# A two-layer hybrid diffusion backbone on one core: waits and orders of the opening and odd stages, and router logits in four column groups with a fold

## The chip, the cores and the metric

The kernel runs on one core of a Trainium2 chip. The metric is the device time of one execution in microseconds (us); lower is better. The core has five engines that run side by side: TensorE (PE in the profile, with its weight loads as PEld), VectorE (DVE), ScalarE (ACT), GpSimd (POOL) and SyncE (SP), which here only issues DMAs. Each engine works through its own instruction stream in order, and streams meet only at semaphores. A wait in a stream therefore also holds back everything behind it in that stream.

## The reference, cut to what matters

```python
for l in range(DEPTH):                                   # DEPTH = 2; 1024 latent and 256 context tokens, D = 1024
    mod = split(s_lat @ ada_w[l] + ada_b[l], 6)          # s_lat = silu(c); the same with s_ctx for the context
    h = modulate(rmsnorm(x, norm_mix_g[l]), mod[0], mod[1])
    if l % 2 == 0:   # even: short gated convolution || bidirectional gated linear attention
        k, v, lr_f, lr_b = split(h @ w_in[:, kv])        # la = log_sigmoid(lr @ decay_up + decay_b) / 16
        ...                                              # b = cumsum of la in chunks of 64; exp(b), exp(-b) scale q, k
    else:            # odd: RG-LRU || spatial gating: mixed = einsum(sg_w, layernorm(gelu(v)))
        ...
    x = x + mod[2] * y
    h = modulate(rmsnorm(x, norm_ffn_g[l]), mod[3], mod[4])
    aff = softmax(h @ w_router)                          # 16 experts; each takes its top-C tokens
    x = x + mod[5] * expert_choice_moe(h, aff, ...)
    ...                                                  # the same for the context in layer 0
return rmsnorm(x_lat, norm_final_g)
```

## The kernel before, in words

The 1280 tokens are ten tiles of 128 (`NT` = 10; eight latent, `TL`, and two of context). All work is one hand-written stream per engine, and the stages follow each other in program order on each of them.

**Opening** (`pe_start` and the start of each engine's block). SP issues fifteen small loads, eight 1 MB pieces of `ada_w` (each 128 rows of 2048) into seven slots, and then four weight units of 512 KB; ACT issues the ten token tiles. PE transposes the small vectors, waits for the silu of the conditioning vectors, and then alternates per tile between eight transposes of a normalised tile (`norm_transposes`, L542) and one `ada` piece (L487). ACT computes squares and roots (`act_square`, L1399, and `act_root`, L819) and copies half of each transposed tile (L853); VectorE takes the reciprocal, scales the tile (`dve_norm`, L906 and L909), and copies the other half (L858). After the tiles, VectorE makes the low halves of four weight units (`dve_weight_low`, L899), copies the modulation sums out of PSUM (`dve_ada_rows`, L919), PE transposes them (`ada_rows`, L496), and VectorE adds the bias and makes the scales (`dve_ada_columns`, L936 and L946). Only then can ACT write the high parts of the modulated features (`act_h_high`, L871) and VectorE their low parts (`dve_h_low`, L882 and L890). PE's `job_pair` (L591 to L593) follows them chunk by chunk: each product is three fp32r matmuls, high by high, low by high and high by low.

**Decays and value tiles of the even layer.** PE makes four decay projections (L630). For each of them VectorE runs `dve_decay_in` (L982, L985), ACT an exp and a log with a table load before each (L975, L976), and VectorE `dve_decay_out` (L993 and a scan, L995 or L997). PE then makes 20 value tiles (`v_tile`, L603 to L605, 24 matmuls each), which alternate between PSUM banks 6 and 7: value tile x waits for the copy of tile x-2, which VectorE makes at L2363. In VectorE's stream all 20 copies stand behind the last `dve_decay_out`.

**Output projection and router** (`pe_wout`, `act_wout`, `dve_wout`, one loop over the tiles in each layer). In step i PE projects tile i (48 matmuls, L783 to L785), transposes the normalised tile i-1 (L542), computes the router logits of tile i-2 (eight fp32 matmuls, L798, with the 128x128 features as the stationary operand and 16 columns of the router moving), and transposes the affinities of tile i-3 (L806). VectorE takes the maximum of the logits (L1272), ACT their exp (L1342). After the last tile VectorE ranks tokens (L1292 to L1297), which gives the experts their tokens. In layer 0 PE also does sixteen late `ada_w` pieces after the loop.

**Odd layer** (`pe_odd`, `act_odd`, `dve_odd`). PE transposes ten tiles, then the four 128x128 spatial weights into PSUM bank 7 (L1949), and then waits for `spatial_weights_copied` before `job_pair`. That copy (L2011) stands in ACT's stream behind all 24 instructions of `act_h_high`. The pair writes PSUM banks 0 to 5; the value tiles, later in the stage, write banks 6 and 7.

## Time and profile before

| what | us |
|---|---|
| median of 3 runs | 2715.66 (2715.24 to 2718.46) |
| profiled execution, its own time | 2716.58 |
| span of the profiled execution | 2714.9 |
| PE busy in the span | 2404.2 |
| DVE busy | 1799.7 |
| ACT busy | 1419.0 |

The page cuts the span into 40 slices and gives for each the busy share of an engine in tenths and the clock that TensorE was granted, also in tenths of full speed. Further views list instructions in order of time, with their duration and the idle time in brackets before them with what ended it; the waits of an engine, summed by what they waited for; and the issues and rates of the DMAs.

### The profile page before, as it was taken

To read this page: it belongs to the slowest core of one execution; us is meant where nothing else is said; L and a number is where in the kernel's file an instruction comes from. 1 tells how busy PE (TensorE), PEld (TensorE's weight loads), DVE (VectorE), ACT (ScalarE), POOL (GpSimd) and SP (SyncE) were. 2 spreads that over 40 slices of the span, in tenths; PEclk is the share of its full clock that TensorE was granted. 3 is DMA by queue.
4 is the path that set the end of the run, shared out by engine and by line. 5 is a ranking of instruction groups with operands and counts; after the bars stand their busy time and mean duration, and the time that the engine had idled before them with its cause. 6 is when DMAs were issued, how large, how long until landed. Compare 5 with 4: busy or idle time off the path is not lost.

```text
span 2714.9 us, 33815 instructions
## 1 busy us (share of the span) xinstructions
PE 2404.2 (89%) x13000; PEld 1835.9 (68%) x13000; DVE 1799.7 (66%) x1986; ACT 1419.0 (52%) x1423; POOL 185.8 (7%) x220
## 2 busy tenths in 40 slices
PE   4799999769958999999999967998792899999994
PEld 3697777658815666666666646777582688888883
DVE  5512121554467788888888755566547799999995
ACT  6400102663415566666666643465441677777774
POOL 0000000000001011110101000000000011111100
PEclk8899999789958999999999977999895899999997
DMA  6014443204374788787778760111333799999995
GB/s 234 24 55 140 151 139 130 117 17 163 140 287 162 297 289 296 288 299 294 286 293 289 281 194 20 36 35 28 133 133 138 281 385 391 389 390 390 389 382 196
DMA packets 186995, 582.35 MB, mean 215 GB/s; under 512 B 13208, under 2 KB 58000, under 8 KB 180496
## 3 DMA queue, kind: packets, MB, share of 16 engines
q1 hardware_dynamic: 171488, 526.43, 51.7%
q0 software_dynamic: 12192, 48.24, 6.5%
q10 hardware_dynamic: 3216, 6.29, 0.6%
q8 instruction: 70, 1.15, 0.2%
q14 instruction: 29, 0.24, 0.0%
HBM read 533.74 MB, written 47.19 MB: 214 GB/s over the span
## 4 chain that ended last, share of the span: by engine, by line
PE 83%; DVE 7%; ACT 4%; DMA 3%; issue 2%; SPq 0%; POOL 0%; POOLq 0%; ACTq 0%; DVEq 0%
PE ps L1503 14%; PE ps L1504 13%; PE ps L1505 13%; PE ps L1516 6%; PE ps L566 5%; PE ps L567 4%; PE ps L568 4%; PE ps L783 2%; PE ps L785 2%; PE ps L784 2%; PE ps L487 1%; PE ps L542 1%; PE ps L798 1%; PE ps L603 1%; PE ps L604 1%
## 5 line engine op out<-in xcount | busy, mean ns | idle before, releaser
L1716 DVE TENSOR_TENSOR R_H_r<-R_M,R_W_r 128x2048 fp32r<-128x2048 f32 x336 | 761.7, 2288 | 145.7 <-ACT R_W_r L1619 145.6
L1619 ACT CAST R_W_r<-R_M 128x2048 fp32r<-128x2048 f32 x336 | 640.2, 1913 | 221.3 <-PE ps L1505 84.3
L1505 PE MATMUL ps<-R_W_r,R_C_r 128*128 128x512 f32 x1536 | 607.2, 395 | 0.0
L1503 PE MATMUL ps<-R_W_r,bc_r 128*128 128x512 f32 x1024 | 413.1, 403 | 13.0 <-DVE R_C_r L1734 9.5
L1504 PE MATMUL ps<-R_H_r,bc_r 128*128 128x512 f32 x1024 | 405.3, 396 | 0.0
L1505 PEld LDWEIGHTS ps<-R_W_r,R_C_r 128*128 128x128 f32 x1536 | 291.0, 189 | 65.1
L566 PE MATMUL ps<-R_H_r,R_W_r 128*128 128x512 f32 (+1 forms) x632 | 234.7, 371 | 16.6 <-DVE R_W_r L899 8.9
L1503 PEld LDWEIGHTS ps<-R_W_r,bc_r 128*128 128x128 f32 x1024 | 194.0, 189 | 70.2 <-issue 16.4
L567 PE MATMUL ps<-R_C_r,R_W_r 128*128 128x512 f32 (+1 forms) x632 | 230.4, 365 | 0.0
L568 PE MATMUL ps<-R_H_r,R_W_r 128*128 128x512 f32 (+1 forms) x632 | 229.7, 363 | 0.0
L1504 PEld LDWEIGHTS ps<-R_H_r,bc_r 128*128 128x128 f32 x1024 | 194.2, 190 | 41.4
L1503 PE MATMUL ps<-R_W_r,R_M_r 128*128 128x512 f32 x512 | 202.3, 395 | 7.0 <-DVE R_C L1806 4.5
L1504 PE MATMUL ps<-R_H_r,R_M_r 128*128 128x512 f32 x512 | 202.0, 395 | 0.0
L899 DVE TENSOR_TENSOR R_W_r<-R_W,R_W_r 128x1024 fp32r<-128x1024 f32 x41 | 49.7, 1223 | 172.9 <-ACT R_W_r L895 172.6
L566 PEld LDWEIGHTS ps<-R_H_r,R_W_r 128*128 128x128 f32 x632 | 120.3, 190 | 57.4 <-issue 30.7
L895 ACT CAST R_W_r<-R_W 128x1024 fp32r<-128x1024 f32 x41 | 42.6, 1047 | 213.7 <-DMA R_W<-in_ev_w_in 199.6
L1516 PE MATMUL ps<-R_M,R_C 128*32 128x512 f32 x1344 | 154.2, 596 | 0.0
L568 PEld LDWEIGHTS ps<-R_H_r,R_W_r 128*128 128x128 f32 x632 | 120.4, 191 | 19.0
L567 PEld LDWEIGHTS ps<-R_C_r,R_W_r 128*128 128x128 f32 x632 | 120.6, 191 | 17.2
L783 PE MATMUL ps<-R_H_r,R_M_r 128*128 128x512 f32 x288 | 115.3, 400 | 15.9 <-DVE R_C_r L1238 15.9
L1503 PEld LDWEIGHTS ps<-R_W_r,R_M_r 128*128 128x128 f32 x512 | 97.8, 191 | 40.5 <-issue 19.8
L1716 DVE TENSOR_TENSOR R_H_r<-R_H,R_W_r 128x2048 fp32r<-128x2048 f32 x48 | 109.8, 2288 | 12.9 <-ACT R_W_r L1619 12.9
(291 smaller groups left out, 3734.1 us busy)
## 6 DMA issues: line engine op xcount, KB each, us to landing
R_M<-in_moe_w_gate SPq DMA_DIRECT2D x114, 1024.0 KB, 8.3
R_M<-in_moe_w_down SPq DMA_DIRECT2D x112, 1024.0 KB, 7.8
R_M<-in_moe_w_up SPq DMA_DIRECT2D x110, 1024.0 KB, 7.5
bc<-in_ada_w SPq DMA_DIRECT2D x24, 1024.0 KB, 4.9
R_H<-in_moe_w_up SPq DMA_DIRECT2D x18, 1024.0 KB, 11.1
R_W<-in_ada_w SPq DMA_DIRECT2D x16, 1024.0 KB, 7.5
R_H<-in_moe_w_down SPq DMA_DIRECT2D x16, 1024.0 KB, 10.2
R_H<-in_moe_w_gate SPq DMA_DIRECT2D x14, 1024.0 KB, 9.6
```

Source lines behind the costliest of these rows:

```text
L566: pe.matmul(o, wh[:, k, :], tokens_of(R_Hr, k, c0, cn), start=(k == 0), stop=False)
L567: pe.matmul(o, wh[:, k, :], tokens_of(R_Cr, k, c0, cn), start=False, stop=False)
L568: ins = pe.matmul(o, wl[:, k, :], tokens_of(R_Hr, k, c0, cn), start=False, stop=(k == KC - 1))
L783: pe.matmul(o, xh, whi_out[:, k, cs], start=(k == 0), stop=False)
L784: pe.matmul(o, xh, wlo_out[:, k, cs], start=False, stop=False)
L785: ins = pe.matmul(o, xl, whi_out[:, k, cs], start=False, stop=(k == KC - 1))
L1503: pe.matmul(o, hi[:, k, :], wh[:, kk, cs], start=(k == 0), stop=False)
L1504: pe.matmul(o, hi[:, k, :], wl[:, kk, cs], start=False, stop=False)
L1505: ins = pe.matmul(o, lo[:, k, 0:P], wh[:, kk, cs], start=False, stop=(k == KC - 1))
L1516: ins = pe.matmul(ps[32 * q:32 * q + C, cbank, :], full[:, 2 * j + kk, P:P + C], w[:, kk, c * BANK:(c + 1) * BANK], start=(j == 0), stop=( ...
L1619: nc.scalar.copy(whi[j], raw[slot + j]).then_inc(unit_high_done, 1)
L1716: nc.vector.tensor_tensor(wlo[j], raw[slot + j], whi[j], ALU.subtract).then_inc(unit_low_done, 1)
```

## The change

Six edits:

- The router's 16 columns per 128 rows are stored 32 apart, with zeros between (a memset on POOL at the start). The features now move (128 columns) and a 128x32 piece of the router is stationary. The eight pieces go to four column groups of TensorE, two to each, and so leave four partial sums of the logits on 128 partitions, transposed. ACT copies them out of PSUM, and one more matmul with `fold` (four 16x16 identities below each other) adds the four parts and turns them back. In the loop this fold is issued one step later, after the first twelve matmuls of the next projection; in the last steps at once.
- In the opening, ACT squares and roots tile 0 before the silu, and the exp and log of the LRU constants move behind the decays; VectorE's use of them moves with them. VectorE builds `fold` in three small adds.
- VectorE copies the modulation sums before the weight units' low halves, and makes two of these (not four) before the modulation columns.
- VectorE's copies of value tiles 0 to 4 are put between the steps of the decays.
- In the odd layer PE waits for the spatial weights' copy only before the first value tile.
- The reads of the logits (L1272, L1342) move to columns 128 to 143 of the same PSUM bank.

```diff
@@ pe_wout
+            def logits_folded(t):
+                pe.wait_ge(logit_parts_copied, r0 + t + 1)
+                pe.matmul(ps[:, 2, P:P + NE], logit_parts[:, :], fold[:, :], start=True, stop=True).then_inc(logits_done, 1)
...
                     for k in range(KC):
+                        if i >= 3 and k == 2:
+                            logits_folded(i - 3)
...
                     for k in range(KC):
-                        ins = pe.matmul(ps[:, 2, 0:NE], hN[l][t % 2][:, k, :], router[:, k * NE:(k + 1) * NE],
-                                        start=(k == 0), stop=(k == KC - 1))
-                    ins.then_inc(logits_done, 1)
+                        q = 32 * (k % 4)
+                        ins = pe.matmul(ps[q:q + 32, 2, 0:P], router3[:, k, :], hN[l][t % 2][:, k, :], start=(k < 4), stop=(k >= 4))
+                    ins.then_inc(logit_parts_done, 1)
+                    if i >= nt - 1:
+                        logits_folded(t)
@@ act_wout, behind act_blocks and ahead of act_square
+                if 2 <= i <= nt + 1:
+                    t = i - 2
+                    act.wait_ge(logit_parts_done, r0 + t + 1)
+                    act.wait_ge(logits_done, r0 + t)
+                    nc.scalar.copy(logit_parts[:, :], ps[:, 2, 0:P]).then_inc(logit_parts_copied, 1)
@@ pe_odd
-            pe.wait_ge(spatial_weights_copied, 1)
...
+                    if b == 0:
+                        pe.wait_ge(spatial_weights_copied, 1)
@@ scalar block
+            act.wait_ge(constants_made, 4)
+            tile_in(act, 0)
+            act_square(act, 0)
+            act_root(act, 0)
             act.wait_ge(vectors_copied, 1)
...
-            act.wait_ge(lru_constants_done, 1)
-            own.do(nc.scalar.activation(lruc[:, 8:16], lruc[:, 8:16], ACT.Exp, scale=-1.0))
-            nc.scalar.activation(lruc[:, 8:16], lruc[:, 8:16], ACT.Ln, bias=1.0).then_inc(lambda_log_done, 1)
@@ vector block
+            dve_ada_rows(dve, 0)
-            for u in range(4):
+            for u in range(2):
                 dve_weight_low(dve, u)
-            dve_ada_rows(dve, 0)
             dve_ada_columns(dve, 0)
```

In the opening, on VectorE, the rows before are these (L858 copies the last tiles, L899 are the four low halves, L919 the copies of the modulation sums, L936 and L946 the columns):

```order
L858 COPY R_C<-ps 128x4x128 [waits normed_transposed] x2
L899 TENSOR_TENSOR R_W_r<-R_W,R_W_r 128x1024 [waits weight_high_done] x4
L919 COPY bc<-ps 2x512 [waits constants_made,ada_unit_used]
L919 COPY bc<-ps 2x512 x3
L936 TENSOR_TENSOR modc<-ps,adab 128x16 [waits ada_rows_transposed]
```

and now, with L872, L913, L933 and L950 in their places:

```order
L872 COPY R_C<-ps 128x4x128 [waits normed_transposed] x2
L933 COPY bc<-ps 2x512 [waits constants_made,ada_unit_used]
L933 COPY bc<-ps 2x512 x3
L913 TENSOR_TENSOR R_W_r<-R_W,R_W_r 128x1024 [waits weight_high_done] x2
L950 TENSOR_TENSOR modc<-ps,adab 128x16 [waits ada_rows_transposed]
```

The copies of the sums moved ahead of the low halves, and two of these moved behind the features' low parts.

In the decays, on VectorE, the rows before from the third `dve_decay_in` on (L993 with the scans L995 and L997 is `dve_decay_out`, L2363 the value tiles' copy):

```order
L982 TENSOR_SCALAR R_M<-ps,vcol 128x1280 [waits job_done]
L985 SCALAR_TENSOR_TENSOR R_W<-R_M 128x1280 [waits job_emptied_by_vector]
L993 SCALAR_TENSOR_TENSOR R_W<-R_M,R_W 128x1280 [waits decay_log_done,constants_made]
L995 SCALAR_TENSOR_TENSOR R_M<-bc,R_W 128x1280 [waits vector_own]
L982 TENSOR_SCALAR R_M<-ps,vcol 128x1280 [waits job_done]
L985 SCALAR_TENSOR_TENSOR R_W<-R_M 128x1280 [waits job_emptied_by_vector]
L993 SCALAR_TENSOR_TENSOR R_W<-R_M,R_W 128x1280 [waits decay_log_done,constants_made]
L997 SCALAR_TENSOR_TENSOR R_M<-bc,R_W 128x1280 [waits vector_own]
L993 SCALAR_TENSOR_TENSOR R_W<-R_M,R_W 128x1280 [waits decay_log_done,constants_made]
L997 SCALAR_TENSOR_TENSOR R_M<-bc,R_W 128x1280 [waits vector_own]
L2363 COPY R_M<-ps 128x256 [waits v_tile_done] x15
```

and now (L996 and L999 are `dve_decay_in`, L1007 and L1009 or L1011 `dve_decay_out`, L1017 the copy), up to the last `dve_decay_out`:

```order
L996 TENSOR_SCALAR R_M<-ps,vcol 128x1280 [waits job_done]
L999 SCALAR_TENSOR_TENSOR R_W<-R_M 128x1280 [waits job_emptied_by_vector]
L1017 COPY R_M<-ps 128x256 [waits v_tile_done]
L1007 SCALAR_TENSOR_TENSOR R_W<-R_M,R_W 128x1280 [waits decay_log_done,constants_made]
L1009 SCALAR_TENSOR_TENSOR R_M<-bc,R_W 128x1280 [waits vector_own]
L1017 COPY R_M<-ps 128x256 [waits v_tile_done]
L996 TENSOR_SCALAR R_M<-ps,vcol 128x1280 [waits job_done]
L999 SCALAR_TENSOR_TENSOR R_W<-R_M 128x1280 [waits job_emptied_by_vector]
L1017 COPY R_M<-ps 128x256 [waits v_tile_done]
L1007 SCALAR_TENSOR_TENSOR R_W<-R_M,R_W 128x1280 [waits decay_log_done,constants_made]
L1011 SCALAR_TENSOR_TENSOR R_M<-bc,R_W 128x1280 [waits vector_own]
L1017 COPY R_M<-ps 128x256 [waits v_tile_done] x2
```

Five copies now stand ahead of the last `dve_decay_out`, and fifteen behind it.

In the odd layer, on PE, before (L1949 transposes the spatial weights, L591 opens the pair):

```order
L1949 MATMUL ps<-ident,R_M 128x128 x3
L591 MATMUL ps<-R_H_r,R_W_r 128x512 [waits job_emptied_by_scalar,job_emptied_by_vector,weight_low_done,spatial_weights_copied,h_low_done,h_written_by_scalar,h_written_by_vector]
L592 MATMUL ps<-R_H_r,R_W_r 128x512
```

and now (L596 opens the pair, L608 the first value tile, 340 rows later):

```order
L1973 MATMUL ps<-ident,R_M 128x128 x3
L596 MATMUL ps<-R_H_r,R_W_r 128x512 [waits job_emptied_by_scalar,job_emptied_by_vector,weight_low_done,h_low_done,h_written_by_scalar,h_written_by_vector]
L597 MATMUL ps<-R_H_r,R_W_r 128x512
...
L608 MATMUL ps<-R_W_r,R_H_r 128x256 [waits weight_low_done,spatial_weights_copied]
```

The wait for the copied spatial weights left the pair and stands on the first value tile.

## Rows read from the trace of the kernel before

**Rows 1.** The page: busy time of PE, and its granted clock in slices.
```profile
PE 2404.2 (89%) x13000; PEld 1835.9 (68%) x13000; DVE 1799.7 (66%) x1986; ACT 1419.0 (52%) x1423; POOL 185.8 (7%) x220
PEclk8899999789958999999999977999895899999997
```

**Rows 2.** Waits of PE, first 190 us: for whom, sum, times, longest.
```profile
PE ps L603 <- DVE R_M L2363: 12.2, 1, 12.2
PE ps L496 <- DVE bc L919: 9.0, 1, 9.0
PE ps L542 <- DVE R_W L909: 8.5, 2, 7.5
```

**Rows 3.** Opening: start, us, engine, line, operation, [idle before]; DMA rate in 1.5 us slices.
```profile
15.62 1.28 ACT L2288 ACT_TABLE_LOAD   x1
19.47 0.29 ACT L819 ACTIVATE st<-st,epsc 128x1 f32<-128x1 f32 x1
20.89 1.94 PE L542 MATMUL ps<-ident,R_W 128*128 128x128 f32 x8 [7.48 <-DVE R_W L909]
38.79 1.04 PE L487 MATMUL ps<-R_M,silc 128*2 128x512 f32 x8
GB/s 0 213 399 261 372 382 398 392 429 399 442 407 412 415 415 421 431 415 418 426 410 426 431 400 309 295 291 290 247 53 0 0 0 0 0 0 0 5 0 0
```

**Rows 4.** Instructions in time, DVE and ACT, modulation rows and columns.
```profile
44.59 4.63 DVE L899 TENSOR_TENSOR R_W_r<-R_W,R_W_r 128x1024 fp32r<-128x1024 f32 x4 [0.87 <-ACT R_W_r L895]
49.14 2.78 DVE L919 COPY bc<-ps 2x512 f32<-2x512 f32 x4
53.13 0.26 DVE L936 TENSOR_TENSOR modc<-ps,adab 128x16 f32<-128x16 f32 x2 [1.21 <-PE ps L496]
```

**Rows 5.** Instructions in time, DVE and PE, decays and value tiles.
```profile
118.63 1.52 DVE L982 TENSOR_SCALAR R_M<-ps,vcol 128x1280 f32<-128x1280 f32 x1
120.19 1.49 DVE L985 SCALAR_TENSOR_TENSOR R_W<-R_M 128x1280 f32<-128x1280 f32 x1
121.60 1.48 DVE L993 SCALAR_TENSOR_TENSOR R_W<-R_M,R_W 128x1280 f32<-128x1280 f32 x1
123.11 2.82 DVE L995 TENSOR_TENSOR_SCAN R_M<-bc,R_W 128x1280 f32<-128x1280 f32 x1
137.78 0.58 PE L603 MATMUL ps<-R_W_r,R_H_r 128*128 128x256 f32 x1 [12.21 <-DVE R_M L2363]
148.68 0.42 DVE L2363 COPY R_M<-ps 128x256 f32<-128x256 f32 x1 [2.46 <-PE ps L605]
```

**Rows 6.** Instructions in time, one step of the router's loop, and an expert stage.
```profile
673.35 1.86 PE L798 MATMUL ps<-router,R_H 128*128 128x16 f32 x16
675.06 0.27 PE L806 MATMUL ps<-ident,sm 128*16 128x128 f32 x1
676.37 0.16 DVE L1272 TENSOR_REDUCE st<-ps 128x1 f32<-128x16 f32 x1
673.55 1.50 ACT L835 ACTIVATE R_H<-ps,modc,scg 128x128 f32<-128x128 f32 x4 [6.57 <-PE ps L542]
877.33 3.64 PE L1516 MATMUL ps<-R_M,R_C 128*32 128x512 f32 x32
880.90 0.51 PE L1503 MATMUL ps<-R_W_r,bc_r 128*128 128x512 f32 x1
878.22 0.13 PEld L1516 LDWEIGHTS ps<-R_M,R_C 128*32 128x32 f32 x4 [0.30 <-issue]
```

**Rows 7.** Instructions in time, PE, behind layer 0's last projection.
```profile
748.77 3.43 PE L798 MATMUL ps<-router,R_H 128*128 128x16 f32 x16
753.15 3.57 PE L798 MATMUL ps<-router,R_H 128*128 128x16 f32 x16 [0.73 <-ACT sm L1342]
```

**Rows 8.** Instructions in time, start of the odd layer's pair: DVE, PE.
```profile
1640.55 0.68 DVE L890 TENSOR_TENSOR R_C_r<-R_C,R_H_r 128x512 fp32r<-128x512 f32 x1
1654.54 0.77 PE L591 MATMUL ps<-R_H_r,R_W_r 128*128 128x512 f32 x1 [15.97 <-DVE R_C_r L890]
```

More of the change, by code:

```diff
@@ L94, in build @@
         st = sb("st", 64)
-        router = sb("router", KC * NE)
+        router = sb("router", KC * 32)
+        router3 = router[:, :].rearrange("p (k e) -> p k e", e=32)
+        fold = sb("fold", NE)
+        logit_parts = sb("logit_parts", P)
         dec = sb("dec", 4 * NCH)
@@ L403, in build @@
         normed_stored = sem("normed_stored")
+        logit_parts_done = sem("logit_parts_done")
+        logit_parts_copied = sem("logit_parts_copied")
         logits_done = sem("logits_done")
@@ L998, in dve_decay_out, with dve_v_copied @@
             ins.then_inc(decays_summed, 1)
+        def dve_v_copied(dve, x):
+            half, t = divmod(x, NT)
+            dve.wait_ge(v_tile_done, x + 1)
+            nc.vector.tensor_copy(vtok[:, t, 256 * half:256 * half + 256], ps[:, 6 + x % 2, 0:256]).then_inc(v_tile_copied, 1)
         def dve_even_job(dve, own, j):
@@ L1271, in dve_wout @@
                     dve.wait_ge(logits_done, r0 + t + 1)
-                    own.do(nc.vector.reduce_max(st[:, b:b + 1], ps[:, 2, 0:NE], AXX))
+                    own.do(nc.vector.reduce_max(st[:, b:b + 1], ps[:, 2, P:P + NE], AXX))
                     nc.vector.tensor_scalar(st[:, b + 1:b + 2], st[:, b:b + 1], -1.0, None, ALU.mult).then_inc(logit_max_done, 1)
@@ L1341, in act_wout @@
                         act.wait_ge(affinities_transposed, r0 + t - 1)
-                    nc.scalar.activation(sm[:, s0:s0 + NE], ps[:, 2, 0:NE], ACT.Exp, bias=st[:, b + 1:b + 2],
+                    nc.scalar.activation(sm[:, s0:s0 + NE], ps[:, 2, P:P + NE], ACT.Exp, bias=st[:, b + 1:b + 2],
                                          accum_out=st[:, b + 2:b + 3]).then_inc(logit_exps_done, 1)
@@ L1392, in sp_wout @@
                 if i == 0:
-                    sp.dma_start(router[:, :].rearrange("p (k e) -> p k e", e=NE),
+                    sp.dma_start(router3[:, :, 0:NE],
                                  I["moe_router"][l].rearrange("(k p) e -> p k e", p=P)).then_inc(lowrank_weights_loaded, 16)
@@ L2176, in _ @@
             pool.wait_ge(constants_made, 1)
+            own.do(pool.memset(router[:, :], 0.0))
             pool.memset(decup[96:128, :], 0.0).then_inc(constants_made, 1)
@@ L2284, in _ @@
                 nc.scalar.activation(s3[:, :, w], vcol[:, VEC[name]:VEC[name] + KC], ACT.Silu).then_inc(cond_silu_done, 1)
[L2286 to L2289 removed]
             for t in range(NT + 1):
[L2291 removed]
+                if 1 <= t < NT:
                     tile_in(act, t)
@@ L2304, in _ @@
                 act_decay(act, own, jobs[j][1])
+            act.wait_ge(lru_constants_done, 1)
+            own.do(nc.scalar.activation(lruc[:, 8:16], lruc[:, 8:16], ACT.Exp, scale=-1.0))
+            nc.scalar.activation(lruc[:, 8:16], lruc[:, 8:16], ACT.Ln, bias=1.0).then_inc(lambda_log_done, 1)
             for u in range(index["cg0"], index["cg0"] + 2):
@@ L2334, in _ @@
             own.do(nc.vector.tensor_scalar(lruc[:, 0:8], lam, -1.0, 0.0, ALU.mult, ALU.max))
-            dve.wait_ge(lambda_log_done, 1)
-            own.do(nc.vector.tensor_tensor(lruc[:, 0:8], lruc[:, 0:8], lruc[:, 8:16], ALU.add))
-            nc.vector.tensor_scalar(lruc[:, 16:24], lruc[:, 0:8], -LRU_C, None, ALU.mult)
-            nc.vector.tensor_scalar(lruc[:, 0:8], lruc[:, 0:8], LRU_C, None, ALU.mult).then_inc(lru_constants_done, 1)
+            dve.wait_ge(constants_made, 1)
+            own.do(nc.vector.tensor_tensor(fold[:, :], ident[:, 0:NE], ident[:, 32:32 + NE], ALU.add))
+            own.do(nc.vector.tensor_tensor(fold[:, :], fold[:, :], ident[:, 64:64 + NE], ALU.add))
+            own.do(nc.vector.tensor_tensor(fold[:, :], fold[:, :], ident[:, 96:96 + NE], ALU.add))
             for t in range(NT + 1):
@@ L2349, in _ @@
             dve_h_low(dve, own, 0)
-            for u in range(4, 7):
+            for u in range(2, 7):
                 dve_weight_low(dve, u)
-            for pd in range(4):
-                dve_decay_in(dve, pd)
-                if pd >= 1:
-                    dve_decay_out(dve, own, pd - 1)
-            dve_decay_out(dve, own, 3)
-            for x in range(2 * NT):
-                half, t = divmod(x, NT)
+            dve_decay_in(dve, 0)
+            dve_decay_in(dve, 1)
+            dve_decay_out(dve, own, 0)
+            dve_decay_in(dve, 2)
+            dve_v_copied(dve, 0)
+            dve_decay_out(dve, own, 1)
+            dve_v_copied(dve, 1)
+            dve_decay_in(dve, 3)
+            dve_v_copied(dve, 2)
+            dve_decay_out(dve, own, 2)
+            dve_v_copied(dve, 3)
+            dve_v_copied(dve, 4)
+            dve_decay_out(dve, own, 3)
+            dve.wait_ge(lambda_log_done, 1)
+            own.do(nc.vector.tensor_tensor(lruc[:, 0:8], lruc[:, 0:8], lruc[:, 8:16], ALU.add))
+            nc.vector.tensor_scalar(lruc[:, 16:24], lruc[:, 0:8], -LRU_C, None, ALU.mult)
+            nc.vector.tensor_scalar(lruc[:, 0:8], lruc[:, 0:8], LRU_C, None, ALU.mult).then_inc(lru_constants_done, 1)
+            for x in range(5, 2 * NT):
                 if x == NT + 5:
@@ L2361, in _ @@
                         dve_weight_low(dve, u)
-                dve.wait_ge(v_tile_done, x + 1)
-                nc.vector.tensor_copy(vtok[:, t, 256 * half:256 * half + 256], ps[:, 6 + x % 2, 0:256]).then_inc(v_tile_copied, 1)
+                dve_v_copied(dve, x)
             for i in range(len(even_late)):
```

2 lines of the change are left out of this document (removed).

## The prediction

> **What bounds the kernel now.** I read the page's engine shares first: PE is busy for 2404.2 of 2714.9 us, the others for at most 1800 [rows 1]. Outside PE's own work there are some 310 us in which it waits, and the slices of its granted clock dip to 0.7 or 0.8 of full speed around the same places. So an edit is worth what it takes from PE's waits, or from PE's work where PE never waits. Then I read the list of PE's waits over the first 190 us: one wait of 12.2 us for the copy of a value tile, one of 9.0 us for the copy of the modulation sums, and 8.5 us for the first normalised tiles [rows 2]. The instructions in order of time give the rest: in the router's loop PE has no idle time, and at the odd layer's pair it waits 15.97 us [rows 8]. These are the four places that the change touches. Every stage behind them is released by semaphores alone, so time won at one of them should move all that follows.
>
> **Opening, the first tile.** ACT now finishes tile 0's root early; before, it came at 19.76, behind the exp and log of the LRU constants, each with a table load of 1.28 us [rows 3]. VectorE is then ready at about 15: its constants end at 14.2 and the three fold adds cost 0.2 each. The scaling takes 0.8, and PE's first transposes start at 15.8 instead of 20.89, 5.1 us earlier. Tile 1's root has to follow the silu and one more table load, which puts it at about 16.9, and that is before PE has done tile 0 (twice 1.9 us at half clock). But those 5.1 us do not arrive at the end. PE also needs the eight 1 MB pieces, and the DMA rate is near its plateau of 400 GB/s from 3 to 36 us [rows 3]. Added up slice by slice, the 13.6 MB of tiles and pieces are in at 36 us at the earliest and at about 37.5 with the weight units between them; the last piece was used at 38.79. So this edit gives 1.3 to 2.6 us, and nothing if PE's waits for pieces keep its clock at half. I take 1.7. What hides the rest is the DMA, and if the pieces came faster the cover would be gone and 5 us be won.
>
> **Opening, the sums before the low halves.** Before, the four low halves (4.63 us from 44.59) stood ahead of the copies of the sums (2.78 us), and the columns came at 53.13 [rows 4]. Now the copies start when the last tile is copied, at 43.7, and end at 46.5. PE transposes the sums for 1.1 us beside the first of two low halves (1.16 each), and the columns follow at 48.8. That is 4.3 us won. The two low halves taken away from here run behind the features' low parts, where VectorE had nothing to do; the pair needs only the first two. SP's queue is unchanged. The opening as a whole: 4.3 + 1.7 = **6.0 us**, from 4.0 to 6.9.
>
> **Decays and value tiles.** In the trace PE has value tiles 0 and 1 ready at 125.57 and then stands until 137.78 because tile 0's copy is behind all decays; tile 2 then starts at half clock (matmuls of 0.21 apart instead of 0.12, about 5.1 us for the tile instead of the 2.88 between two copies, which is 0.42 + 2.46) [rows 5]. Up to the end of the third `dve_decay_in` at 121.6 nothing changes. Tile 0 is ready at 122.5, so its copy goes in at 122.6 to 123.0. Then comes `dve_decay_out` (1.48 + 2.82, 4.3 us) until 127.3, copy 1 until 127.8, `dve_decay_in` (3.0) until 130.8, copy 2 until 131.2, `dve_decay_out` until 135.5, copies 3 and 4 until 136.3. PE runs tile 2 from 125.5, tile 3 from 128.4, tile 4 from 131.3 to 134.2, waits some 1.7 us for copy 3, and runs tile 5 from 135.9 and tile 6 from 138.8. The last `dve_decay_out` ends at 140.6, and the constants (three small operations, 0.6) at 141.2, just before tile 6 ends at 141.7. ACT's exp and log with their table loads (5.1 us per decay) fit between, and those of the constants end near 138. So tile 7 starts at 141.7, and the last of the 20 ends 13 x 2.88 later at 179.1; before, it was 137.8 + 5.1 + 17 x 2.88 = 191.9. That gives **12.6 us**. The bounds are 11 (copies that slip by half a microsecond each, PE once more at half clock for 1 us) and 13.2. The wait for all four decays in SP's queue ends 3 us later, at 140.6; behind it is the load of an `ada_w` piece that PE needs at 184, so nobody notices.
>
> **Router, in the loop.** The eight logit matmuls are 16 records and hold PE for 1.71 us per tile (673.35 to 675.06) [rows 6]. No row shows 32 stationary columns with 128 moving ones. The nearest are the context's matmuls in the expert stage, with 512 moving in the same four column groups: four records per 0.43 us, so the groups do run side by side [rows 6]. Scaled to 128 columns that is 0.11 per four, but four weight loads alone take 0.13, so 16 records take 0.43 to 0.52. Entering and leaving the mode costs 0.16: the block of 32 records lasts from 877.33 to 880.90, 3.57 where 8 x 0.43 is 3.41 [rows 6]. From above the price is bounded by today's 1.71, if the groups run one after the other. I take 0.7, nearest to the context's rows. The fold is one matmul of the old form, a 128x128 stationary with 16 columns, 1.71 / 8 = 0.21, and 0.3 with its entry into the fp32r stream. Net 1.71 - 0.7 - 0.3 = 0.7 per tile, between -0.3 and 1.1. This counts where PE is the bound, seven tiles of layer 0 and five of layer 1: 12 x 0.7 = **8.5 us**, between -3.6 and 13.
>
> The new wait on PE is the fold's, and the rest of a projection is queued behind it. PE reaches it twelve matmuls (2.7 us) into the projection, at about 676.9 in the step of the rows. ACT begins the copy when its blocks end, at 675.05 [rows 6], and needs 0.4 us, so 1.4 us are spare. VectorE's maximum comes 0.6 us later than at 676.37, and its chain up to the scaled tile with it; PE asks for that tile some 7 us later. ACT's square comes 0.4 us later, with the same cover.
>
> The Trainium skill speaks against the change here. TensorEngine Tiling (Array Packing), section Key Properties: changing the tiling mode drains the engine. The rows show 0.16 us for a way in and out. If a drain at each of the two changes cost a whole matmul of 0.39 us instead, the parts would be 0.6 us dearer and this kernel 12 x 0.6 = 7 us slower than my sum, some 2680.
>
> **Router, behind the last projection.** Here PE runs at half clock, and logits cost 3.3 to 3.4 us for each of two tiles, one of them waiting for the other's exp [rows 7]. Now I put 1.4 for the parts, 0.4 for ACT's copy, 0.45 for the fold and 0.3 for two handoffs, 2.55 us. For the first of the two, ACT's blocks are late anyway and only 0.3 us are won; the chain to the ranking is 1.25 us shorter in each layer. In layer 0 the late `ada_w` pieces follow and release each other's DMAs, in layer 1 the ranking does, so it counts in both: **2.5 us**, from -3 (dear parts and the handoffs on top) to 4.
>
> **Odd layer.** VectorE's first low part ends at 1641.2, and PE starts at 1654.54, when ACT has finished the 24 high parts and the copy [rows 8]. The list names VectorE as the releaser, but it had long been done. Without that wait the pair starts at 1641.3. It won't be starved: VectorE makes a low part of 512 columns in 1.06 us, and PE needs six matmuls per part, 1.36 us at full and 2.6 at half clock. ACT's copy is done long before the first value tile, which comes behind four projections. So **13.2 us**, between 12 and 13.3. Next late is the weight unit for the fourth projection, whose load is released by the pair itself and moves along.
>
> **Sum.** 6.0 + 12.6 + 8.5 + 2.5 + 13.2 = 42.8 us. The profiled execution took 2716.6 (span 2714.9 and 1.7 around it), 0.9 above the median of the runs; 2715.7 - 42.8 = **2673 us**.
>
> **Rivals.** (a) The column groups run one after the other at 128 columns, the fold comes on top, and the opening gains only its order: -3.6 in the loop, -3 behind it, 4.3 + 12.6 + 13.2 elsewhere, 23.5 us won, 2692. For it: no row has this shape, and weight loads may not hide. Against: the context's block. (b) The copies between the decays pay less, because PE's 1.7 us wait takes its clock down and tiles 5 to 7 run at half (3 x 2.2 us): 6.6 less, 2680. For it: the clock fell in the wait at 125.6; against: that one was seven times longer. (c) The parts cost only 0.45 and the fold 0.2, and the opening gives its 6.9: 12 x 0.35 + 1 + 1.5 more, 2666. (d) **Slower:** the fold's wait opens a gap in each projection, and PE's clock stays at half through the loop. A projection is 48 matmuls of 0.23 at full and 0.43 at half clock, so 9.6 us dearer. Without the router's gain 32 us are won elsewhere, and three or four of twelve tiles at half clock eat them; all twelve give 2716 - 32 + 115 = 2799. Against it stands the 1.4 us of spare time. (e) The waits do go, but a stage behind gives part of it back through something I don't see: 2690 to 2716.
>
> **How the numbers follow.** Chances: the sum as worked, 2668 to 2679, 0.60; (a) 0.10; (b), and the drain's price, 0.12; (c) 0.10; (d) 0.03; (e) 0.05. The range has the first, (b), (c) and part of (a): 2664 to 2690. A measurement of this kernel can tell about 0.2% (5.4 us) from no change. Faster by more than that is all but (d) and a part of (e): 0.95; same 0.02; slower 0.03.
>
> **What would show it.** The first transposes near 15.8 and the columns at 46 to 49; value tile 2 directly behind tile 1 and an idle time before tile 5 of 1 to 2.5 us; the parts at 0.5 to 0.9 us per tile, a step of the loop at 12.9 instead of 13.6, and no idle time before the fold; the odd pair's first matmul within 4 us of the last spatial transpose. I am wrong if a step of the loop is no shorter, if PE waits for the fold, or if the pair waits for features.

## The result, and the profile after

The changed kernel takes **2673.4 us** (median of four runs, 2671.5 to 2677.9) where the kernel before takes 2715.9 (2715.2 to 2718.5, four runs of it beside these): a ratio of 0.9844 with a 95% interval of 0.9827 to 0.9861. The same kernel in a later comparison gave 2673.8 against 2715.9, 0.9848 (0.9834 to 0.9861). The prediction was 2673.0, in a range of 2664 to 2690. Its profiled execution took 2673.8 us, with a span of 2672.1.

The page of the kernel after: PE has 36 more records and 20 us less busy time, and its clock is at about the same height as before [rows 1].

```profile
PE 2384.4 (89%) x13036; PEld 1802.6 (67%) x13036; DVE 1800.7 (67%) x1989; ACT 1424.7 (53%) x1443; POOL 186.3 (7%) x221
PEclk9899999889859999999999988999895999999997
```

PE's waits of the kernel after in the first 190 us (for whom, sum, times, longest). They answer to [rows 2], and the three waits shown there have shrunk: the value tiles' from 12.2 to 1.5, the sums' from 9.0 to 3.5, the tiles' from 8.5 to 2.9. The wait for the first loads, which no edit touches, heads the list as it did before (12.8 us then). New are waits for the pieces of `ada_w` (L492).

```profile
PE ps L616 <- DMA bc<-in_ada_b: 13.2, 1, 13.2
PE ps L596 <- DVE R_C_r L904: 4.7, 1, 4.7
PE ps L492 <- DMA R_M<-in_ada_w: 3.9, 6, 1.1
PE ps L501 <- DVE bc L933: 3.5, 1, 3.5
...
PE ps L547 <- DVE R_W L923: 2.9, 2, 2.5
PE ps L608 <- DVE R_M L1017: 1.5, 1, 1.5
```

The opening after, PE and then VectorE in order of time (start, us, engine, line, operation, the idle time before it in brackets). The first transposes start at 16.36 instead of 20.89 and the last pieces of `ada_w` are used at 37.73 instead of 38.79 [rows 3]; the sums stand ahead of two low halves, and the columns come at 47.14 instead of 53.13 [rows 4].

```profile
16.36 1.94 PE L547 MATMUL ps<-ident,R_W 128*128 128x128 f32 x8 [2.52 <-DVE R_W L923]
37.73 1.04 PE L492 MATMUL ps<-R_M,silc 128*2 128x512 f32 x8 [0.56 <-DMA R_M<-in_ada_w]
41.95 2.78 DVE L933 COPY bc<-ps 2x512 f32<-2x512 f32 x4
47.14 0.26 DVE L950 TENSOR_TENSOR modc<-ps,adab 128x16 f32<-128x16 f32 x2
```

One step of the router's loop after, PE and ACT in order of time. L811 are the parts, L820 the transpose of the affinities, L778 the fold and L1353 ACT's copy. They answer to the 1.71 us of the logits in [rows 6]. The row of the fold has no idle time in brackets, and ACT's copy (end 641.75) had been ready for 1.7 us.

```profile
639.98 0.64 PE L811 MATMUL ps<-R_H,router 128*32 128x128 f32 x16
640.56 0.28 PE L820 MATMUL ps<-ident,sm 128*16 128x128 f32 x1
643.45 0.29 PE L778 MATMUL ps<-fold,logit_parts 128*128 128x16 f32 x2
651.86 1.03 PE L547 MATMUL ps<-ident,R_W 128*128 128x128 f32 x8
652.83 0.64 PE L811 MATMUL ps<-R_H,router 128*32 128x128 f32 x16
```

```profile
641.47 0.28 ACT L1353 COPY logit_parts<-ps 128x128 f32<-128x128 f32 x1
```

The odd layer after, PE in order of time: the last of the four spatial transposes, and the pair's first matmul 2.81 us behind it, where it was 15.97 [rows 8].

```profile
1611.51 1.06 PE L1973 MATMUL ps<-ident,R_M 128*128 128x128 f32 x4
1615.38 0.77 PE L596 MATMUL ps<-R_H_r,R_W_r 128*128 128x512 f32 x1 [2.81 <-DVE R_C_r L904]
```

Where the 42.8 us between the two profiled executions come from, by the start of the same instruction in both traces ("between" is what lies outside the stretch named with it):

| up to | before | after | gained so far | by this stretch |
|---|---|---|---|---|
| first modulation columns | 53.13 | 47.14 | 6.0 | 6.0 |
| last value tile's copy | 191.88 | 173.70 | 18.2 | 12.2 |
| ranking, layer 0 | 759.16 | 732.36 | 26.8 | 7.8 router, 0.8 between |
| spatial transposes, layer 1 | 1637.52 | 1611.51 | 26.0 | -0.8 |
| last matmul of L591 (now L596) in the odd pair | 1683.35 | 1644.00 | 39.3 | 13.3 |
| ranking, layer 1 | 2059.16 | 2013.17 | 46.0 | 6.5 router, 0.2 between |
| last gathered tokens transposed | 2607.51 | 2562.83 | 44.7 | -1.3 |
| last expert added | 2681.26 | 2638.25 | 43.0 | -1.7 |

So the edits brought 46, and the experts of layer 1 took 3 back. The experiments undo the parts one by one, and then look for those 3.

### The profile page after: what moved, and what is told of

The parts are those of the page before. It is cut to its first block, busy times and chain, and to the rows that moved or that the text cites. A ratio compares the mean times of both kernels' runs of the same rounds, so it can differ in the third digit from the quotient of the medians.

```text
span 2672.1 us, 33931 instructions
## 1 busy us (share of the span) xinstructions
PE 2384.4 (89%) x13036; PEld 1802.6 (67%) x13036; DVE 1800.7 (67%) x1989; ACT 1424.7 (53%) x1443; POOL 186.3 (7%) x221
## 4 chain that ended last, share of the span: by engine, by line
PE 83%; DVE 6%; ACT 4%; DMA 4%; issue 2%; SPq 0%; POOL 0%; POOLq 0%; ACTq 0%; DVEq 0%
PE ps L1527 14%; PE ps L1529 13%; PE ps L1528 13%; PE ps L1540 6%; PE ps L571 5%; PE ps L572 4%; PE ps L573 4%; PE ps L795 3%; PE ps L797 2%; PE ps L796 2%; PE ps L492 1%; PE ps L1548 1%; DMA R_W<-in_ada_w 1%; PE ps L608 1%; PE ps L547 1%
## 5 line engine op out<-in xcount | busy, mean ns | idle before, releaser
L913 DVE TENSOR_TENSOR R_W_r<-R_W,R_W_r 128x1024 fp32r<-128x1024 f32 x41 | 49.6, 1221 | 165.8 <-ACT R_W_r L909 165.2
```

## Experiments

Each edit is made to the changed kernel unless it is said otherwise; "the new kernel" is the changed one. Ratios are to the kernel before on the same chip. Three to five rounds leave about 4 us of uncertainty on a difference of two such medians, so a small effect is read from the time of a fixed instruction in the trace, and the medians only have to agree with it. Traces spread too: where nothing was edited, the time between two fixed instructions differs from one profile to the next by up to 3 us in the opening, by as much in layer 0 behind its ranking, and by up to 2 us in the odd layer.

**The router's old product.**

```
-    q = 32 * (k % 4)
-    ins = pe.matmul(ps[q:q + 32, 2, 0:P], router3[:, k, :], hN[l][t % 2][:, k, :], start=(k < 4), stop=(k >= 4))
+    ins = pe.matmul(ps[:, 2, P:P + NE], hN[l][t % 2][:, k, :], router3[:, k, 0:NE], start=(k == 0), stop=(k == KC - 1))
     (and no fold, no copy of the parts)
```

> The new kernel with the router's old product alone: h tiles stationary, eight matmuls of 16 columns per tile straight into the logits, no parts, no copy by ScalarE, no fold. Theory (the router gives a little every step and the rest in each layer's last steps): the time rises by about 14 us, to some 2687.6; the router's group of a step lasts 1.35 us again instead of 0.58 + 0.29, a step takes 13.6 us instead of 12.84, and the moves of the opening and of the odd layer are untouched (value copy of the last tile at 173.7, odd pair's gain in place). Layer 0's share 7.8, layer 1's 6.5. Rival one (the groups are a small part, the fold's cover does it elsewhere): under 8 us. Rival two (part of the gain was given back in layer 1's expert stage by something the router's earlier end triggers there, 2.9 us): then that stage, 76.6 us in the new kernel, is 73.9 again here and the time rises by 11 only.

Measured: 2687.3 us, ratio 0.9888 (0.9872 to 0.9905), about 12 above the new kernel. PE in order of time shows the old group and the old step, 669.30 - 655.70 = 13.60 us:

```profile
655.70 1.86 PE L808 MATMUL ps<-router,R_H 128*128 128x16 f32 x16
668.43 1.03 PE L547 MATMUL ps<-ident,R_W 128*128 128x128 f32 x8
669.30 1.86 PE L808 MATMUL ps<-router,R_H 128*128 128x16 f32 x16
```

From the first logits to the ranking it takes 7.8 us more than the new kernel in layer 0, and 6.5 more in layer 1. The router's share holds, 14 us. The second rival fell: an expert of layer 1 takes 35.05 us here too, as in the new kernel, so what was given back there isn't set off by the router's work.

**The value copies behind the decays.**

```
+            for pd in range(4):
+                dve_decay_in(dve, pd)
+                if pd >= 1:
+                    dve_decay_out(dve, own, pd - 1)
+            dve_decay_out(dve, own, 3)
-            (the twelve calls with copies 0 to 4 between them)
```

> The new kernel with VectorE's four decays ahead of all ten value copies again. Theory (the value projection waits for its banks, each freed by one copy): PE's wait ahead of value tile 2 is about 13 us again, the copy of the last value tile ends at 185.9 instead of 173.7, and the kernel takes 12.2 us more, 2685.6. Rival (other work of the first stage, ScalarE's decays or the weight transfers, was nearly as late, so that the copies' order is worth less than it shows): under 9 us.

Measured: 2689.7 us, ratio 0.9897 (0.9881 to 0.9914). The wait is back on PE, and between the pair's start and the last value tile the kernel is 12.2 us slower than the new one:

```profile
131.23 0.58 PE L608 MATMUL ps<-R_W_r,R_H_r 128*128 128x256 f32 x1 [12.78 <-DVE R_M L1017]
```

The medians say 14 to 16, at the edge of their uncertainty, and this profile ends 15.0 us behind the new kernel's. The surplus lies between the ranking of layer 0 and the spatial transposes, 882.8 us here for 879.2 in the new kernel. Two more profiles, of the late root and of the uncovered fold, have it (882.9 and 882.2), the other eleven have 877.5 to 880.1. At least half of it comes ahead of the first expert's result. Its cause stays open, so "time won at one place moves all that follows" is exact only to some 3 us there.

**The odd layer's wait ahead of the pair.**

```
+            pe.wait_ge(spatial_weights_copied, 1)
             j = n_even_jobs
...
-                    if b == 0:
-                        pe.wait_ge(spatial_weights_copied, 1)
```

> The new kernel with PE's wait for the odd layer's spatial weights back ahead of the whole pair of projections. Theory: PE stands idle for 16 us there instead of 2.9, and the kernel takes 13.3 us more, 2686.7. Rival (the late start is partly caught up by later stages that have slack, as layer 1's experts): under 11 us, with the difference gone by the end of the experts.

Measured: 2687.6 us, ratio 0.9892 (0.9875 to 0.9908). PE stands 16.4 us, and the pair starts 13.2 us later than in the new kernel. The delay isn't caught up: the ranking of layer 1 comes 14.3 later and the last expert 14.5. At the spatial transposes this kernel was only 0.1 behind. The other 1.3 came between the pair and layer 1's first logits, a stretch that takes 318.0 to 320.3 us in the fourteen profiles without going with any edit. That rival fell too.

```profile
1611.58 0.60 PE L1973 MATMUL ps<-ident,R_M 128*128 128x128 f32 x4
1628.55 0.77 PE L596 MATMUL ps<-R_H_r,R_W_r 128*128 128x512 f32 x1 [16.38 <-DVE R_C_r L904]
```

**The four low halves ahead of the sums.**

```
-            dve_ada_rows(dve, 0)
-            for u in range(2):
+            for u in range(4):
                 dve_weight_low(dve, u)
+            dve_ada_rows(dve, 0)
             dve_ada_columns(dve, 0)
-            for u in range(2, 7):
+            for u in range(4, 7):
```

> The new kernel with VectorE's four low halves of weights ahead of the two copies of modulation rows again. Theory (the rows wait behind low halves that nobody needs yet, and PE's first pair waits for them): the columns of the modulation are ready about 4.3 us later, the pair starts at 54.9 instead of 50.6, and the kernel takes 4.3 us more, 2677.7. Rival one (the wait only changes its name: PE then waits for low halves): the pair's start moves by under 2 us and the time by as little. Rival two (the early root of tile 0 carries the opening): also under 2 us.

Measured: 2681.0 us, ratio 0.9868 (0.9852 to 0.9884). PE waits 9.1 us for the sums instead of 3.5, the columns come 3.8 later and the pair 4.0, and the last expert is 4.2 later than in the new kernel: nothing of it is made up on the way. The clean size is the time from the end of VectorE's copy of the last tile to the columns: 9.4 to 9.5 us in the three profiles with the old order (the kernel before, its copy with 64 bytes more, and this one), 5.1 to 5.2 in all others, so 4.3 us. VectorE in order of time:

```profile
42.34 4.70 DVE L913 TENSOR_TENSOR R_W_r<-R_W,R_W_r 128x1024 fp32r<-128x1024 f32 x4 [0.87 <-ACT R_W_r L909]
46.95 2.78 DVE L933 COPY bc<-ps 2x512 f32<-2x512 f32 x4
50.94 0.26 DVE L950 TENSOR_TENSOR modc<-ps,adab 128x16 f32<-128x16 f32 x2 [1.21 <-PE ps L501]
```

**The late root.**

```
-            act.wait_ge(constants_made, 4)
-            tile_in(act, 0)
-            act_square(act, 0)
-            act_root(act, 0)
             act.wait_ge(vectors_copied, 1)
...
+            act.wait_ge(lru_constants_done, 1)
+            own.do(nc.scalar.activation(lruc[:, 8:16], lruc[:, 8:16], ACT.Exp, scale=-1.0))
+            nc.scalar.activation(lruc[:, 8:16], lruc[:, 8:16], ACT.Ln, bias=1.0).then_inc(lambda_log_done, 1)
```

> The new kernel with ScalarE's exp and ln of the lambda constants ahead of the tiles' roots again, and the first tile's square and root behind the silu. Theory: the first transposes and the first tile's columns move back by about 1.7 us and the kernel by as much, 1.7 more than the new one (the step's own term in the prediction). Rival (the root of tile 0 is off the path: PE is held by the weights' transfers and the rows' copies): the pair of projections starts within 0.5 us of the new kernel's 50.6, and the time doesn't move.

Measured: 2677.2 us, ratio 0.9852 (0.9835 to 0.9868), which the runs can't tell from the new kernel. The trace can at its start: the first transposes begin at 20.84 instead of 16.36, 4.5 us later, and the pair at 52.5 instead of 50.6, 1.8 us. So of 4.5 us at tile 0 some 2.7 are gone before the pair. That the transfers of `ada_w` hide them shows in PE's waits: in all eleven profiles with the early root it waits for pieces, at the longest 1.1 to 2.2 us in one go, and with the late root (here and in both traces of the old kernel) never. The 1.8 us themselves are not firm: of the ten profiles in which the new opening is left as it is, nine have the pair at 49.7 to 51.6 us and one at 53.0, later than here. (From the ranking of layer 0 on this profile lies some 4 us further off, with nothing of the edit in it; that says nothing on the root.)

```profile
20.84 1.94 PE L547 MATMUL ps<-ident,R_W 128*128 128x128 f32 x8 [7.55 <-DVE R_W L923]
```

**The fold without its cover.**

```
-                        if i >= 3 and k == 2:
-                            logits_folded(i - 3)
...
-                    if i >= nt - 1:
-                        logits_folded(t)
+                    logits_folded(t)
```

> The new kernel with the fold always directly behind its tile's parts, as it stands now only for each layer's last three tiles. Theory (the fold is cheap because the next tile's transposes cover ScalarE's copy; without the cover PE waits for it): a wait of 0.7 to 1.2 us for ScalarE ahead of each of the twelve further folds, 8 to 14 us more. Rival (ScalarE copies at once and the pipeline of PE's records hides it): under 3 us. The prediction's slower case would show here too: if such gaps bring the granted clock to half, the stage between the projections takes far more than 14 us.

Measured: 2691.2 us, ratio 0.9907 (0.9891 to 0.9924), some 17 above the new kernel. PE waits for the parts' copy ten times between 600 and 760 us, 10.5 us in all, where the new kernel has three such waits, 2.3 us, at its last three folds. Each fold in the loop shows it:

```profile
PE ps L778 <- ACT logit_parts L1350: 10.5, 10, 1.2
```

```profile
642.20 0.64 PE L809 MATMUL ps<-R_H,router 128*32 128x128 f32 x16
644.02 0.40 PE L778 MATMUL ps<-fold,logit_parts 128*128 128x16 f32 x2 [1.18 <-ACT logit_parts L1350]
```

A step takes 14.06 us instead of 12.84, times twelve 14.6. That makes the router dearer than its old form (13.60 a step): all of its gain in the loop hangs on where the fold stands. The rest of the 17 us is the surplus in layer 0 told above, 3 us in this profile. The granted clock stayed at 1.00 from 652 to 722 us in spite of a gap of 1.18 us in each step, so a wait of this length doesn't bring the prediction's slower case.

**One column group.**

```
-    q = 32 * (k % 4)
-    ins = pe.matmul(ps[q:q + 32, 2, 0:P], router3[:, k, :], hN[l][t % 2][:, k, :], start=(k < 4), stop=(k >= 4))
+    ins = pe.matmul(ps[0:32, 2, 0:P], router3[:, k, :], hN[l][t % 2][:, k, :], start=(k == 0), stop=(k == KC - 1))
     (the copy of the parts and the fold over 32 partitions)
```

> The new kernel with all eight parts of a tile in one group of 32 columns, one behind the other, and the fold over 32 rows. Theory (the four groups work side by side, 0.58 us for the 16 records): one group serialises them at about 0.106 us each, 1.7 us a tile: 1.1 us more for each of the twelve tiles in the loop, 13 us, and up to 2.3 us more for each of the six last tiles at the half clock, so 13 to 27 us in all. Rival (the groups bring nothing and the gain is that of the 32 columns loaded instead of 128): the parts take 0.58 us here as well and the time stays.

Measured: 2697.0 us, ratio 0.9931 (0.9915 to 0.9947), 23.5 above the new kernel. The same sixteen records, with the same shape, in one group:

```profile
642.84 1.94 PE L810 MATMUL ps<-R_H,router 128*32 128x128 f32 x16
657.27 1.93 PE L810 MATMUL ps<-R_H,router 128*32 128x128 f32 x16
```

They last 1.94 us where four groups need 0.64, and a step takes 14.43 us: with no groups the new form would be 0.8 us a step *worse* than the old. In the medians, 12 x 1.6 = 19 us of the 23.5 lie in the loops and the rest behind them. This is the mechanism of rival (a) made real, and it shows that the overlap of the groups carries the router's gain. The Trainium skill, TensorEngine Tiling (Array Packing), Key Properties, says that different tiles can load weights and multiply in parallel; this pair of runs agrees, 0.64 against 1.94 us.

**The three microseconds given back.** In layer 1 the experts follow one another at a fixed distance. VectorE's addition of each expert's result in order of time, of the kernel before and then of the one after:

```profile
2284.67 1.28 DVE L1743 SCALAR_TENSOR_TENSOR R_W<-ps,gcolT,bc 128x1024 f32<-128x1024 f32 x1
2319.61 1.28 DVE L1743 SCALAR_TENSOR_TENSOR R_W<-ps,gcolT,bc 128x1024 f32<-128x1024 f32 x1
```

```profile
2239.03 1.28 DVE L1767 SCALAR_TENSOR_TENSOR R_W<-ps,gcolT,bc 128x1024 f32<-128x1024 f32 x1
2274.07 1.28 DVE L1767 SCALAR_TENSOR_TENSOR R_W<-ps,gcolT,bc 128x1024 f32<-128x1024 f32 x1
```

That is 34.94 us before and 35.04 after, every time, with no idle time on PE in the distance looked at (2274 to 2309 us before, 2228 to 2263 after) and its clock at 1.00 in both. All seven experiments above have the same 35.05. The instructions are the same, but the tiles aren't where they were: the router's tile grew by 512 bytes a partition and `fold` (64 bytes) and `logit_parts` (512) came in behind it, so that all later tiles moved by 1088 bytes. The first test puts them back:

```
-        router = sb("router", KC * 32)
-        router3 = router[:, :].rearrange("p (k e) -> p k e", e=32)
-        fold = sb("fold", NE)
         logit_parts = sb("logit_parts", P)
...
         R_W, R_Wr = sb_twice("R_W", 11264)
+        router = sb("router", KC * 32)
+        router3 = router[:, :].rearrange("p (k e) -> p k e", e=32)
+        fold = sb("fold", NE)
```

> The new kernel's instructions, with the router's enlarged tile and the fold's matrix allocated behind all other tiles and the parts' tile in the router's old place, so that every other tile has the address of the kernel before. Open point: from layer 1's second expert on, each expert takes 35.05 us in the new kernel and in four variants of it, 34.94 in the kernel before, with the same instructions and the clock at full; and the last 12.5 us of its experts run at a mean clock of 0.88 in the new kernel and those variants, 1.00 before. Theory: the addresses of the tiles, moved by 1088 bytes, cost the 0.11 us per expert (1.4 us in all); here an expert takes 34.94 us and the time falls by about 1.4 us, or by 3 if the clock's dip goes too. Rival: it is not the addresses (the program's code or the phase of the transfers): 35.05 us stay and so does the time.

Measured: 2670.4 us (2669.2 to 2672.5), ratio 0.9831 (0.9817 to 0.9844). An expert takes 34.94 us again:

```profile
2239.70 1.28 DVE L1767 SCALAR_TENSOR_TENSOR R_W<-ps,gcolT,bc 128x1024 f32<-128x1024 f32 x1
2274.64 1.28 DVE L1767 SCALAR_TENSOR_TENSOR R_W<-ps,gcolT,bc 128x1024 f32<-128x1024 f32 x1
```

Then two single runs ask which part of the move costs. With only `fold` behind the other tiles (`fold = sb("fold", NE)` moved below `R_W`), the tiles stand 1024 bytes from their old places:

> The new kernel with the fold's matrix alone (64 bytes a partition) behind the other tiles: these stand 1024 bytes from where they stood before instead of 1088. If it is the odd 64 bytes that cost, layer 1's experts take 34.94 us; if any move costs, 35.05.

```profile
2238.43 1.28 DVE L1767 SCALAR_TENSOR_TENSOR R_W<-ps,gcolT,bc 128x1024 f32<-128x1024 f32 x1
2273.36 1.28 DVE L1767 SCALAR_TENSOR_TENSOR R_W<-ps,gcolT,bc 128x1024 f32<-128x1024 f32 x1
```

34.93 us (single time 2671.9). And the kernel *before*, with nothing but an unused tile of 64 bytes behind the router's (`spare = sb("spare", NE)`):

> The kernel before with one unused tile of 64 bytes a partition behind the router's, so that all later tiles stand 64 bytes further. If the odd 64 bytes cost, layer 1's experts take 35.05 us instead of 34.94 and the kernel 1.4 us more than before; if something else of the change does, 34.94.

```profile
2288.15 1.28 DVE L1744 SCALAR_TENSOR_TENSOR R_W<-ps,gcolT,bc 128x1024 f32<-128x1024 f32 x1
2323.19 1.28 DVE L1744 SCALAR_TENSOR_TENSOR R_W<-ps,gcolT,bc 128x1024 f32<-128x1024 f32 x1
```

35.04 us. So it is the odd 64 bytes, and it needs nothing else of the change: 0.11 us for each of twelve experts, and as much in the two shorter distances behind them, some 1.5 us. Which operand minds its address wasn't tried. Layer 0's experts go the same way: from the first result to the last they take 690.4 to 690.9 us in the four kernels without the odd 64 bytes and 691.4 to 692.1 in the ten with them, which would account for the -0.8 in the table. The single time of this run, 2722.1 us, is 6.2 above 2715.9; its last expert comes 6.2 later than before, of which these two stages have 2.5 and the clock's dip told next 1.6.

The other 1.5 us are at the very end. PE, last group of the last expert, before and then after, both behind the same idle time of 2.41 us:

```profile
2669.96 0.47 PE L1503 MATMUL ps<-R_W_r,R_M_r 128*128 128x512 f32 x1 [2.41 <-issue]
```

```profile
2625.50 0.77 PE L1527 MATMUL ps<-R_W_r,R_M_r 128*128 128x512 f32 x1 [2.41 <-issue]
2626.07 0.63 PE L1528 MATMUL ps<-R_H_r,R_M_r 128*128 128x512 f32 x1
2626.49 0.63 PE L1529 MATMUL ps<-R_W_r,R_C_r 128*128 128x512 f32 x1
```

Before, the matmuls went on at the full clock (2.4 GHz). After, seven of them run at the half clock (1.2 GHz), 0.42 us apart instead of 0.23, and the last two additions lie 15.99 us apart instead of 14.54. The kernel again, for this and as the mark for the next:

> The new kernel itself, beside the others of this comparison. 42.5 us faster than the kernel before by medians, as the first time (2673.4 to 2715.9); experts of layer 1 at 35.05 us. One theory holds the clock's dip in the last 25 us of the experts for a matter of when that stage comes, the same in each run of this kernel: then it is there again, and the last two results of the experts' sum lie 16 us apart; the other holds it for chance: then 14.6 or 16.

Measured: 2673.8 us (2672.4 to 2677.9), ratio 0.9848. The dip is there again (15.97 us). But of the fourteen profiles of this study twelve have it, among them the kernel before with its 64 bytes; the kernel before itself and the one with one column group (14.57 us) don't. So neither the change nor the addresses decide whether it comes. Seven or eight matmuls are slow each time, in nine profiles from the first behind the gap, in the three of the new kernel without the odd 64 bytes from the seventh. Whether it hangs on when that stage comes or on chance stays open.

**Both, and one copy more.** The tiles behind, and in the value stage copy 3 inside the third `dve_decay_out`:

```
             own.do(nc.vector.scalar_tensor_tensor(out=t, in0=x, scalar=0.0, in1=t, op0=ALU.min, op1=ALU.subtract))
+            for v in between:
+                dve_v_copied(dve, v)
...
-            dve_decay_out(dve, own, 2)
-            dve_v_copied(dve, 3)
+            dve_decay_out(dve, own, 2, (3,))
```

> The tiles behind (as in the run before with the router's tile and fold's matrix at the end), and one value copy more, the fourth, set inside the third decay, ahead of its logarithm-free last steps, instead of behind it. Theory: PE's only wait in the value projection, 1.45 us ahead of tile 5, goes, the last value tile's copy ends 1.4 us earlier, and the time is 1.4 us under that of the tiles behind alone, 4.3 under the new kernel. Rival: PE then waits as long ahead of a later tile, since VectorE has the same work to do until then: no change against the tiles behind alone.

Measured: 2671.2 us (2669.7 to 2672.1), ratio 0.9832 (0.9819 to 0.9845). It is 2.7 us below the new kernel on the same chip, and the runs don't overlap, but the medians don't show it faster than the tiles behind alone (0.9832 against 0.9831). The first row is the new kernel's wait in the value tiles, the second this kernel's:

```profile
130.21 0.39 PE L608 MATMUL ps<-R_W_r,R_H_r 128*128 128x256 f32 x1 [1.45 <-DVE R_M L1017]
```

```profile
135.15 0.39 PE L608 MATMUL ps<-R_W_r,R_H_r 128*128 128x256 f32 x1 [0.93 <-DVE R_M L1019]
```

The wait went to the tile after next and kept two thirds of its length: VectorE has the same work to do until its last decay is out. From the first value copy to the last it takes 55.9 us instead of 56.4, so half a microsecond was won and not the 1.4 of the theory. The rival was right in the main.

## Why the prediction was right, and where its terms were off

- **Bound and places.** The four places named were the four that paid, and undoing each one alone gave its share back in the traces (4.0, 1.8, 12.2, 14, 13.2 us). That time won at one place moves all that follows held between these two profiles to within a microsecond up to layer 1's experts; in three of the experiments 3 to 4 us more were lost between the ranking of layer 0 and the odd layer.
- **Opening, 6.0 predicted, 6.0 measured.** Order of the rows: 4.3, and 4.3 in every pair of profiles. Early root: 1.7 against 1.8 in the run that undoes it. The step that chose "the transfers hide most of it" over "5.1 us won" was the one that mattered, and the late-root run shows it: 4.5 us at the first tile, 1.8 at the pair. That the sum agrees to a tenth is luck, since the pair's start alone spreads by 3 us with the opening unchanged.
- **Decays and value tiles, 12.6 predicted, 12.2 measured.** The idle time ahead of tile 5 is 1.45 us where 1.7 was worked out. The two end times in the prediction, 191.9 and 179.1, are 12.8 apart and not 12.6, so its sum should have been 43.0. Case (b), a clock at half behind the wait, didn't come: the granted clock is 1.00 from 128 to 140 us, and the row behind the wait has 0.39 us where a matmul at the half clock had 0.58 [rows 5].
- **Router in the loop, 8.5 predicted, 9.2 measured** (a step of 12.84 us instead of 13.60, twelve times). The parts last 0.58 us, from 639.98 to 640.56. The way in adds a tenth ahead of them: the transposes start 0.96 us before the parts, and started 0.87 before the old logits (672.48 for 673.35). Together that is 0.67 for the 0.7 estimated, and the fold is left with 0.28 for 0.3. The clearance ahead of the fold, 1.4 us predicted, was 1.7, and the run without the cover puts a price of 1.22 us a step on it.
- **The drain.** Of those 0.67 us the way into the groups and out again can have at most 0.24, since the context's rows scaled leave 0.43 for the records themselves. The Trainium skill, TensorEngine Tiling (Array Packing), Key Properties, says that the engine drains when the tiling mode changes, and gives no price. (The prediction's own 0.16 us for the way in and out is 3.57 less 8 x 0.43; with these rounded numbers it comes to 0.13.) Had it cost a matmul's 0.39 us each way, the parts would have taken 1.2 or more, which no row here shows.
- **Router behind the last projection, 2.5 predicted, 5 measured.** This is the term that was mis-sized: it was put at half of what came. I took 0.3 us for the first of the two tiles, because ACT's blocks were late anyway. The rows show 1.0: from one tile's parts to the next it takes 3.37 us (724.46 to 727.83) where it was 4.38 [rows 7]. For the last tile the sum had 2.55 us for parts, copy, fold and handoffs; here the parts took 1.08 and the fold came 1.46 after their start, some 2 us in all, and 1.5 us were won:

```profile
727.83 1.08 PE L811 MATMUL ps<-R_H,router 128*32 128x128 f32 x16 [0.73 <-ACT sm L1366]
729.29 0.61 PE L778 MATMUL ps<-fold,logit_parts 128*128 128x16 f32 x2 [0.37 <-ACT logit_parts L1353]
```

- **Odd layer, 13.2 predicted, 13.3 measured.** The pair started 2.81 us behind the transposes, for VectorE's low part, as the wait for the copy was the only other one.
- **What cancelled.** The terms came to 46 us and not 42.8; 3 us went back in layer 1's experts. That is case (e), a later stage that gives something back, with a size far under the 17 us or more that it was drawn with. 1.5 us of it belong to the change, through the addresses, and nothing in the prediction looked at these; the rest is the clock's dip, whose cause stays open. So the median, 2673.4 for 2673.0, is closer than the working deserves: two errors of 3 us with opposite signs.

## What to carry to other kernels

Give a small result the orientation in which the wide data moves and the narrow operand sits in column groups, but only if the fold that it needs can stand where other work covers the copy: without that cover the same form was slower than the old one. When waits of several stages are taken away, work out for each what is late next; here that decided between 5.1 and 1.7 us. And when tiles are added, put a small one like the 64 bytes of `fold` behind the large ones, and compare the pitch of a loop that the change does not touch.

## What the runs showed of the hardware

- Moving the large tiles by 64 bytes a partition made each expert of layer 1 0.11 us longer (35.05 for 34.94 us) with the same instructions at the full clock; moving them by 1024 did not. It shows in both kernels: adding 64 bytes to the kernel before brings it, taking them out of the new one takes it away.
- Sixteen records of 32 stationary and 128 moving columns in fp32 took 0.64 us in four column groups and 1.94 in one. Getting into the groups and out again cost at most 0.24 us, an estimate from the parts' 0.67 and the context's scaled 0.43.
- Gaps of 1.18 us in each 14 us step left the granted clock at 1.00. A gap of 2.41 us behind a stretch at a granted clock of 1.00 was followed, at once or after six matmuls, by seven or eight matmuls at half clock in twelve of fourteen profiles, and by none in two.
